# First norm of a two-block model: feature squares summed on GpSimd and ScalarE before the ones-matmul, and the first two weight splits moved

## The chip, the cores and the metric

The kernel runs on one core of one Trainium2 chip. The metric is the device time of one execution in microseconds; shown of the kernel before are three runs, of which the median counts. One more execution was taken with the hardware profiler, and every row below comes from it.

## The reference

Two transformer-like blocks work on 512 tokens of 1024 features, with 16 learned tokens put ahead of them (528 in all) in the first block. What matters here is its beginning:

```
h = concatenate([meta, x], axis=1)              # 528 tokens x 1024 features
def rms_norm(x, g):
    xf = x.astype(float32)
    y = xf * rsqrt(mean(xf * xf, axis=-1) + EPS)
    return y * g
xn = rms_norm(h, norm_mix_g)
proj = einsum('bld,de->ble', xn, w_in)          # q, k, v, forget logits, conv gates
```

After it come attention with a forget gate, a gated convolution, an output projection and an MLP, and then the second block: a state-space mixer, a gated FFN, differential attention and a second FFN. None of that is touched.

## The kernel before

Activations lie with features on the 128 partitions and tokens along the free dimension: `h` has KT = 8 feature tiles of 128 x 528. Every dense weight passes as one of 308 *units*, 128 x 1024 f32 elements (512 KB), brought by SP from `wstream` into two buffers `raw`. For precision each operand is split in two fp32r parts: ScalarE (ACT) writes `w_hi` from `raw` (`split_hi`, L375), VectorE (DVE) writes `w_lo` = `raw` - `w_hi` (`split_lo`, L379), and TensorE (PE) makes three products, hi*hi, hi*lo and lo*hi. Inputs are split the same way: `x_act` (ACT, L459) writes `x_hi` = h * gain, and `x_dve` (DVE, L465) writes `x_lo`.

The norm's factor is not applied to the input. The product is made of h * gain, and the factor `rstd`, one number per token, is multiplied in when a unit is taken out of PSUM (`wide_dve`, L564). So PE can start before the factor is known, but no bank can be emptied before it is. The first 24 units are wide ones (528 tokens, two halves of 264, so two PSUM banks each; `wide_pe`, L555) and alternate between two pairs of banks: unit n waits until unit n-2 has been taken out (`unit_ev`). Unit 0 walks the eight feature tiles k, and waits at each for its `x_lo`.

The sum of squares of the first norm is made so: GpSimd (POOL) squares the feature tiles one by one into two buffers `sq` (L1542), and PE adds them over features with matmuls against a matrix of ones (`first_stat_pe`, L423), two halves for each tile, all accumulating in one PSUM pair. Tiles 0 to 3 come ahead of unit 0, tiles 4 to 7 between the first four k steps of unit 0. Behind its squares POOL clears `aug_q` and `aug_k` (L1544 to L1547); the last of these brings `consts_ok` to 8, for which ACT waits ahead of the square root (`root_act`, L475). DVE then takes the reciprocal (`root_dve`, L480), splits the low part of unit 2, and takes out unit 0.

The order of work is written out by hand for each engine; each engine runs its own instructions in order, and semaphores tie the engines together. SP's first loads are h tiles 0 and 1, `vecs`, `ones`, h tiles 2 and 3, `raw` of unit 0, the rest of h, `raw` of unit 1. From unit 2 on, the load of unit n waits until w_lo of unit n-2 is written (`load_unit`, L364 to L369). ACT's order at the start is x_hi 0, x_hi 1, w_hi of unit 0, x_hi 2, x_hi 3, w_hi of unit 1, x_hi 4 to 7. DVE's is x_lo 0 to 2, w_lo of unit 0, x_lo 3 and 4, w_lo of unit 1, x_lo 5 to 7.

Of the kernel before, what the change touches and what calls it, by code (L numbers as in the profile page):

```python
# [10 lines left out]
ACT = mybir.ActivationFunctionType  # L11
ALU = mybir.AluOpType
# [4 lines left out]
KT = D // P  # L17
# [3 lines left out]
HALF = TOK // 2  # L21
# [103 lines left out]
def build(nc, A, out, ctx):  # L125
# [38 lines left out]
    ones = sb("ones", [P, P])  # L164
# [77 lines left out]
    ps = ctx.enter_context(nc.psum_tensor("ps", [P, 8, SEQ], F32))  # L242
# [52 lines left out]
    pool_did = sem("pool_did")  # L295
    pool = Count(pool_did)
# [74 lines left out]
    def split_hi(e, u):  # L371
        e.wait_ge(raw_in[u.c % 2], 16 * (u.round + 1))
        if not (isinstance(u.i, int) and u.n() < 4):
            e.wait_ge(unit_mm, u.n(-3))
        e.activation(w_hi[:, u.slot, :], raw[:, u.c % 2, :], ACT.Copy).then_inc(hi_ok, 1)  # L375

    def split_lo(e, u):
        e.wait_ge(hi_ok, u.n(1))
        e.tensor_tensor(w_lo[:, u.slot, :], raw[:, u.c % 2, :], w_hi[:, u.slot, :], ALU.subtract)\  # L379
            .then_inc(lo_ok, 1)  # L380
# [23 lines left out]


    STEP = {0: 0, 1: 1, 3: 2, 2: 3, 4: 4, 5: 5, 6: 6, 7: 7, 8: 8}
    SQUARES = {1: 8, 2: 16, 3: 16, 4: 32, 5: 40, 6: 48, 7: 56, 8: 64}
    SUMS = {1: 0, 2: 7, 3: 7, 4: 21, 5: 28, 6: 35, 7: 42, 8: 49}
    SUM_AT = {1: t2[:, 1, 0:SEQ], 2: t2[:, 0, 0:SEQ], 3: t2[:, 1, 0:SEQ], 4: t2[:, 1, 0:SEQ], 5: t2[:, 1, 0:SEQ],
              6: p_raw[:, 0, :], 7: t2[:, 1, 0:SEQ], 8: t2[:, 1, 0:SEQ]}  # L410
# [6 lines left out]

        return SUMS[n] + (2 * (m - 1) + (n == 2) if n in (2, 3) else m - 1)

    def first_stat_pe(e, m):  # L420
        e.wait_ge(sq_ok, m + 1)
        for half in range(2):
            last = e.matmul(ps[:, 4 + half, 0:HALF], ones[:, :], sq[:, m % 2, half * HALF:half * HALF + HALF],  # L423
                            start=(m == 0), stop=(m == KT - 1))
        last.then_inc(stat_mm, 1)

    def square_act(e, n, m, scale=1.0):

        src = h[:, m, REAL]
        if m == 0:  # L430
            e.wait_ge(stat_mm, 7 + STEP[n] if n != 2 else 7 + STEP[1])
            e.activation(SUM_AT[n], src, ACT.Square, scale=scale).then_inc(sq_ok, 1)
        else:
            k = sum_no(n, m)
            ge(e, sum_ok, k - 1)
            e.activation(sq[:, k % 2, 0:SEQ], src, ACT.Square, scale=scale).then_inc(sq_ok, 1)  # L436
# [29 lines left out]
                               ALU.subtract).then_inc(xlo_ok, 1)  # L466

    def root_act(e, n, eps, cols=SEQ):
        e.wait_ge(stat_mm, 8 + STEP[n])
        ge(e, rstd_ok, STEP[n])  # L470
        if cols > SEQ:
            o, i = halves(rt[:, :]), ps[:, 4:6, 0:HALF]
        else:
            o, i = rt[:, 0:cols], ps[:, 4, 0:cols]
        e.activation(o, i, ACT.Sqrt, bias=eps[:, 0:1], scale=1.0 / D).then_inc(rt_ok, 1)  # L475
# [65 lines left out]
    def wide_pe(e, u):  # L541

        e.wait_ge(lo_ok, u.n(1))
        if not (isinstance(u.i, int) and u.n() < 2):
            e.wait_ge(unit_ev, u.n(-1))
        b = 2 * (u.slot % 2)
        for k in range(KT):
            w = slice(k * P, (k + 1) * P)
            if isinstance(u.i, int) and u.n() == 0:
                if k < 4:  # L550
                    first_stat_pe(e, k + 4)
                e.wait_ge(xlo_ok, k + 1)
            for n, (wt, x) in enumerate(((w_hi, x_hi), (w_hi, x_lo), (w_lo, x_hi))):
                for half in range(2):
                    last = e.matmul(ps[:, b + half, 0:HALF], wt[:, u.slot, w],  # L555
                                    x[:, k, half * HALF:(half + 1) * HALF],
                                    start=(k == 0 and n == 0), stop=(k == KT - 1 and n == 2))
        last.then_inc(unit_mm, 1)

    def wide_dve(e, u, to):  # L560

# [967 lines left out]
    @block.gpsimd  # L1529
    def _(e):  # L1530
        e.memset(eps5[:, :], 1e-5).then_inc(consts_ok, 1)
        e.memset(eps6[:, :], 1e-6).then_inc(consts_ok, 1)
        e.memset(eps_o[:, :], 1e-6 / (1.0 - LAM) ** 2).then_inc(consts_ok, 1)
        e.memset(eps_f[:, :], 1e-11).then_inc(consts_ok, 1)
        e.memset(ones_e[:, :], 1e-6).then_inc(consts_ok, 1)
        e.wait_ge(consts_ok, 5)
        for m in range(KT):
            e.wait_ge(h_in[m // 2], 16)
            if m:
                e.wait_ge(sq_ok, m)  # L1540
            ge(e, stat_mm, m - 1)
            e.tensor_tensor(sq[:, m % 2, :], h[:, m, :], h[:, m, :], ALU.mult).then_inc(sq_ok, 1)  # L1542
        e.wait_ge(sq_ok, 8)
        e.memset(aug_q[:, :, :, :], 0.0).then_inc(consts_ok, 1)  # L1544
        e.memset(aug_k[:, :], 0.0).then_inc(consts_ok, 1)
        e.wait_ge(consts_ok, 7)
        e.memset(aug_k[32:40, :], 1.0).then_inc(consts_ok, 1)  # L1547
        e.wait_ge(consts_ok, 8)
        e.memset(qs[:, :, :, :], 0.0).then_inc(qz_ok, 1)
        e.memset(vp[:, :, :, :, :], 0.0).then_inc(vz_ok, 1)  # L1550
        e.memset(vm[:, :, :, :], 0.0).then_inc(vz_ok, 1)
        e.wait_ge(qz_ok, 1)
        e.wait_ge(vz_ok, 2)
        system_pool(e)
        e.wait_ge(unit_ev, 12)
        e.wait_ge(f_ok, 3)
        stage1_pool(e, 0)
        fence(e, 1)
        stage1_pool(e, 1)
        fence(e, 2)  # L1560
        e.wait_ge(hn_lo, 8)
        e.dma_start(b_in_[:, :, :, :], A["ssm_bc"][:, 0:2, :, :]).then_inc(bc_in, 16)
        e.dma_start(c_raw[:, :, :, :], A["ssm_bc"][:, 2:4, :, :]).then_inc(bc_in, 16)
        for m in range(1, KT):
            sum_pool(e, 1, m)
        tables_pool(e)
        e.drain().then_inc(tables_ok, 1)
        matrices_pool(e, 0)
        for m in range(1, KT):
            sum_pool(e, 3, m)  # L1570
            sum_pool(e, 2, m)

        def spread(u, s):
            e.wait_ge(unit_ev, u.n(1))
            m = u.n(-U_SSM)
            for q in range(4):
# [12 lines left out]
        for n in (4, 5, 6):
            for m in range(1, KT):  # L1590
                sum_pool(e, n, m)
        e.wait_ge(h_fin, 16)
        e.dma_start(onehot, A["onehot"]).then_inc(tab_in, 16)

        e.wait_ge(tab_ok, 2)
        e.dma_start(scratch, tab[0:8, :]).then_inc(tab_out, 16)
        e.memset(qs2[:, :, :, :], 0.0).then_inc(qz2_ok, 1)
        e.wait_ge(qz2_ok, 1)
        e.wait_ge(tab_out, 16)
        for p in range(8):  # L1600
            bias_load(e, p)
            if p == 0:
                e.wait_ge(hn_y, 17)
                e.wait_ge(unit_ev, U_KV + 9)
            stage2_pool(e, p)
            if p == 0:
                fence(e, 5)
        fence(e, 6)
        e.wait_ge(hn_lo, 16)
        e.dma_start(p_raw[:, :, :], A["pT"][:, 1, :, :]).then_inc(p_in, 16)  # L1610
        for n in (7, 8):
            for m in range(1, KT):
                sum_pool(e, n, m)

    @block.scalar
    def _(e):

        e.wait_ge(first_in, 32)
        for m in range(KT):
            e.wait_ge(h_in[m // 2], 16)  # L1620
            x_act(e, 0, m, "norm_mix", TOK)
            if m in (1, 3):
                split_hi(e, Unit(m // 2))
        e.wait_ge(consts_in, 16 * 7)
        e.wait_ge(consts_ok, 8)
        root_act(e, 0, eps5, TOK)
# [23 lines left out]
        for m in range(KT):  # L1650
            u = Unit(U_OUT1 + m)
# [13 lines left out]
        for s in range(16):  # L1665
# [4 lines left out]
            else:  # L1670
                m = s - 8
# [74 lines left out]
    def _(e):  # L1746
# [3 lines left out]
        e.tensor_tensor(gain_fs[:, :], vecs[:, k:k + KT], vecs[:, s:s + KT], ALU.mult).then_inc(gain_ok, 1)  # L1750
        for m in range(KT):
            x_dve(e, 0, m, "norm_mix", TOK)
            if m in (2, 4):
                split_lo(e, Unit(m // 2 - 1))
        e.wait_ge(wf_ok, 1)
        e.tensor_tensor(wf_lo[:, :, :], wf[:, :, :], wf_hi[:, :, :], ALU.subtract).then_inc(wflo_ok, 1)
        root_dve(e, 0, TOK)
# [138 lines left out]
    @block.tensor  # L1896
    def _(e):
        e.wait_ge(first_in, 32)
        for m in range(4):
            first_stat_pe(e, m)  # L1900
        units(e, U_QKVB, 4, lambda u, s: wide_pe(e, u), 1)
        f_pe(e)
        units(e, U_CU, 2, lambda u, s: wide_pe(e, u))
# [191 lines left out]
```

## Time and profile before

| what | us |
| --- | --- |
| median of three runs | 2323.01 (2322.71 to 2323.32) |
| the profiled execution, its own time | 2324.46 |
| its span, first to last instruction | 2322.7 |
| PE busy in that span | 2128.9 (92%) |
| DVE, ACT, POOL busy | 1281.0, 819.9, 466.5 |

The span leaves out what the device does around the program, 1.8 us in this execution. PE is the busiest engine and the chain of work that ended last lies on it for 84% of the span. The stretch that the change touches is the first 40 us. All start times below count from the start of the span.

### The profile page before, as it was taken

To read this page: it belongs to the slowest core of one execution; us is meant where nothing else is said; L and a number is where in the kernel's file an instruction comes from. 1 tells how busy PE (TensorE), PEld (TensorE's weight loads), DVE (VectorE), ACT (ScalarE), POOL (GpSimd) and SP (SyncE) were. 2 spreads that over 40 slices of the span, in tenths; PEclk is the share of its full clock that TensorE was granted. 3 is DMA by queue.
4 is the path that set the end of the run, shared out by engine and by line. 5 is a ranking of instruction groups with operands and counts; after the bars stand their busy time and mean duration, and the time that the engine had idled before them with its cause. 6 is when DMAs were issued, how large, how long until landed. Compare 5 with 4: busy or idle time off the path is not lost.

```text
span 2322.7 us, 27094 instructions
## 1 busy us (share of the span) xinstructions
PE 2128.9 (92%) x9788; PEld 1681.1 (72%) x9788; DVE 1281.0 (55%) x1733; ACT 819.9 (35%) x1309; POOL 466.5 (20%) x596
## 2 busy tenths in 40 slices
PE   8999999999999454799999999999977899999999
PEld 8987668888887354687787877665655577877877
DVE  4253356464355698347747466633366467556455
ACT  3123333122235345534424234432144344334233
POOL 4052017970015784010000001100131000000000
PEclk9999989999999777899999999999899899999999
DMA  4220022232322100122222323221100122323222
GB/s 141 90 73 1 1 73 91 91 100 90 100 91 74 35 1 1 65 91 82 91 99 90 109 82 104 89 69 63 59 19 10 46 82 91 109 80 106 79 98 100
DMA packets 48592, 172.16 MB, mean 74 GB/s; under 512 B 5806, under 2 KB 6318, under 8 KB 48492
## 3 DMA queue, kind: packets, MB, share of 16 engines
q1 hardware_dynamic: 47164, 166.46, 21.6%
q0 software_dynamic: 1328, 4.37, 0.6%
q8 instruction: 63, 1.03, 0.2%
q14 instruction: 37, 0.30, 0.0%
HBM read 168.68 MB, written 2.12 MB: 74 GB/s over the span
## 4 chain that ended last, share of the span: by engine, by line
PE 84%; DVE 8%; ACT 5%; issue 2%; POOL 0%; DMA 0%; DVEq 0%; SPq 0%; ACTq 0%; POOLq 0%
PE ps L393 65%; PE ps L555 6%; PE ps L517 2%; ACT sq L1061 2%; PE ps L1390 1%; PE ps L499 1%; DVE t L1075 1%; PE ps L690 1%; ACT u_t L839 1%; PE ps L691 1%; PE ps L711 1%; PE ps L1392 1%; PE ps L1410 1%; ACT t L1458 1%; PE ps L1026 1%
## 5 line engine op out<-in xcount | busy, mean ns | idle before, releaser
L393 PE MATMUL ps<-x_hi,w_hi 128*128 128x512 f32 x1280 | 513.2, 401 | 5.0 <-DVE w_lo L379 4.9
L393 PE MATMUL ps<-x_lo,w_hi 128*128 128x512 f32 x1280 | 507.1, 396 | 0.0
L393 PE MATMUL ps<-x_hi,w_lo 128*128 128x512 f32 x1280 | 506.4, 396 | 0.0
L379 DVE TENSOR_TENSOR w_lo<-raw,w_hi 128x1024 fp32r<-128x1024 f32 x308 | 395.6, 1287 | 165.1 <-ACT w_hi L375 165.1
L375 ACT ACTIVATE w_hi<-raw 128x1024 fp32r<-128x1024 f32 x308 | 321.8, 1049 | 308.0 <-PE ps L393 136.6
L393 PE MATMUL ps<-a_hi,w_hi 128*128 128x512 f32 x928 | 372.0, 401 | 19.1 <-DVEq L360 11.2
L393 PE MATMUL ps<-a_hi,w_lo 128*128 128x512 f32 x928 | 369.6, 398 | 0.0
L393 PE MATMUL ps<-a_lo,w_hi 128*128 128x512 f32 x928 | 369.5, 398 | 0.0
L393 PEld LDWEIGHTS ps<-x_hi,w_hi 128*128 128x128 f32 x1280 | 241.1, 188 | 86.4 <-issue 22.2
L445 POOL TENSOR_TENSOR t<-t,sq 128x512 f32<-128x512 f32 x49 | 71.4, 1456 | 1116.0 <-ACT sq L436 1115.0
L393 PEld LDWEIGHTS ps<-x_lo,w_hi 128*128 128x128 f32 x1280 | 241.3, 189 | 56.8 <-issue 1.7
L393 PEld LDWEIGHTS ps<-x_hi,w_lo 128*128 128x128 f32 x1280 | 241.5, 189 | 56.3
L393 PEld LDWEIGHTS ps<-a_hi,w_hi 128*128 128x128 f32 x928 | 176.8, 191 | 71.3 <-DVEq L360 11.4
L393 PEld LDWEIGHTS ps<-a_hi,w_lo 128*128 128x128 f32 x928 | 176.6, 190 | 42.1
L393 PEld LDWEIGHTS ps<-a_lo,w_hi 128*128 128x128 f32 x928 | 176.8, 191 | 41.6 <-issue 0.5
L811 DVE TENSOR_TENSOR h<-h,ps 128x512 f32<-128x512 f32 x96 | 65.8, 686 | 204.9 <-PE ps L393 204.9
L1131 ACT ACTIVATE t<-t,vecs 128x512 f32<-128x512 f32 x88 | 71.8, 816 | 241.8 <-DVE t L1159 241.8
L1165 DVE SCALAR_TENSOR_TENSOR t<-t,vecs 128x512 f32<-128x512 f32 x88 | 66.2, 752 | 75.2 <-ACT t L1131 75.2
L1159 DVE TENSOR_TENSOR t<-ps,rstd 128x512 f32<-128x512 f32 x88 | 60.8, 691 | 80.1 <-PE ps L393 79.8
L459 ACT ACTIVATE x_hi<-h,vecs 128x512 fp32r<-128x512 f32 (+1 forms) x56 | 40.0, 722 | 121.6 <-DVE h L811 109.7
L555 PE MATMUL ps<-x_hi,w_hi 128*128 128x264 f32 x384 | 79.5, 288 | 0.0
L555 PE MATMUL ps<-x_lo,w_hi 128*128 128x264 f32 x384 | 78.3, 286 | 0.0
(322 smaller groups left out, 2704.7 us busy)
## 6 DMA issues: line engine op xcount, KB each, us to landing
raw<-in_wstream SPq DMA_DIRECT2D x308, 512.0 KB, 3.3
h<-in_xT SPq DMA_DIRECT2D x4, 528.0 KB, 7.3
b_raw<-scratch POOLq DMA_DIRECT2D x8, 256.0 KB, 3.5
out<-h SPq DMA_DIRECT2D x8, 256.0 KB, 2.0
p_raw<-in_pT POOLq DMA_DIRECT2D x2, 512.0 KB, 4.6
b_in_<-in_ssm_bc POOLq DMA_DIRECT2D x1, 512.0 KB, 4.3
c_raw<-in_ssm_bc POOLq DMA_DIRECT2D x1, 512.0 KB, 6.2
vecs<-in_vecs SPq DMA_DIRECT2D x1, 294.0 KB, 3.8
```

The source lines that it names most:

```text
L375: e.activation(w_hi[:, u.slot, :], raw[:, u.c % 2, :], ACT.Copy).then_inc(hi_ok, 1)
L379: e.tensor_tensor(w_lo[:, u.slot, :], raw[:, u.c % 2, :], w_hi[:, u.slot, :], ALU.subtract)\
L393: last = e.matmul(ps[:, bank, :], wt[:, u.slot, w], x[:, k0 + k, 0:SEQ], start=(k == 0 and n == 0), stop=(k == kt - 1 and n == 2))
L445: e.tensor_tensor(SUM_AT[n], SUM_AT[n], sq[:, k % 2, 0:SEQ], ALU.add).then_inc(sum_ok, 1)
L459: e.activation(hi[:, m, 0:cols], src, ACT.Copy, scale=scale).then_inc(xhi_ok, 1)
L517: e.matmul(ps[:, 6 + k % 2, :], (spread1 if k < 8 else spread2)[:, m * P:(m + 1) * P], roots, start=True, stop=True).then_inc(hn_b, 1)
L555: last = e.matmul(ps[:, b + half, 0:HALF], wt[:, u.slot, w], x[:, k, half * HALF:(half + 1) * HALF], start=(k == 0 and n == 0), stop=(k == ...
L811: i = e.tensor_tensor(h[:, m, REAL], h[:, m, REAL], ps[:, u.slot, :], ALU.add)
L1061: e.activation(dst, u_t[32 * j:32 * j + 32, 4 * m + q, :], ACT.Gelu_apprx_tanh).then_inc(ge_ok, 1)
L1131: e.activation(t1[:, s % 2, 0:SEQ], t0[:, s % 2, 2:SEQ + 2], ACT.Identity, bias=vec(f"ffn_b{layer}", c), scale=vec(f"ffn_w{layer}", 88 + c ...
L1159: e.tensor_tensor(t0[:, s % 2, 2:SEQ + 2], ps[:, u.slot, :], rstd[:, 0:SEQ], ALU.mult).then_inc(unit_ev, 1)
L1165: n = dve.did(e.scalar_tensor_tensor(y, t0[:, s % 2, 1:SEQ + 1], vec(f"ffn_w{layer}", 44 + c), y, ALU.mult, ALU.add))
```

## The change

The sum over feature tiles is taken off PE. POOL keeps a running sum `SUM_0` (in `t1[:, 1, :]`): it squares tile 0 straight into it, squares tiles 2, 4 and 6 into `sq[:, 0, :]`, and ACT squares tiles 1, 3, 5 and 7 into `sq[:, 1, :]`; POOL adds each of the seven to the sum. ACT's square of tile m waits for POOL's sum over tile m-2, since both use one buffer. One pair of matmuls against ones, behind unit 0, adds over the partitions. On ACT, w_hi of unit 1 goes behind everything else of this stage; on DVE, w_lo of unit 0 goes ahead of x_lo 2, and w_lo of unit 1 behind x_lo 7. The counts of `sq_ok` and `stat_mm` in later norms are lowered to match and say nothing new.

```diff
+    SUM_0 = t1[:, 1, :]
+    def first_square_act(e, m):
+        if m > 1:
+            e.wait_ge(sum0_ok, m - 1)
+        e.activation(sq[:, 1, :], h[:, m, :], ACT.Square).then_inc(sq0_ok, 1)
+    def first_sum_pool(e, m):
+        if m == 0:
+            e.tensor_tensor(SUM_0, h[:, m, :], h[:, m, :], ALU.mult).then_inc(sum0_ok, 1)
+            return
+        if m % 2:
+            e.wait_ge(sq0_ok, m // 2 + 1)
+        else:
+            e.wait_ge(sum0_ok, m - 1)
+            n = pool.did(e.tensor_tensor(sq[:, 0, :], h[:, m, :], h[:, m, :], ALU.mult))
+            e.wait_ge(pool_did, n)
+        e.wait_ge(sum0_ok, m)
+        e.tensor_tensor(SUM_0, SUM_0, sq[:, m % 2, :], ALU.add).then_inc(sum0_ok, 1)
-    def first_stat_pe(e, m):
-        e.wait_ge(sq_ok, m + 1)
+    def first_stat_pe(e):
+        e.wait_ge(sum0_ok, KT)
         for half in range(2):
-            last = e.matmul(ps[:, 4 + half, 0:HALF], ones[:, :], sq[:, m % 2, half * HALF:half * HALF + HALF],
-                            start=(m == 0), stop=(m == KT - 1))
+            last = e.matmul(ps[:, 4 + half, 0:HALF], ones[:, :], SUM_0[:, half * HALF:half * HALF + HALF],
+                            start=True, stop=True)
         last.then_inc(stat_mm, 1)
...
-                if k < 4:
-                    first_stat_pe(e, k + 4)
                 e.wait_ge(xlo_ok, k + 1)
...
         last.then_inc(unit_mm, 1)
+        if isinstance(u.i, int) and u.n() == 0:
+            first_stat_pe(e)
...
         for m in range(KT):
             e.wait_ge(h_in[m // 2], 16)
-            if m:
-                e.wait_ge(sq_ok, m)
-            ge(e, stat_mm, m - 1)
-            e.tensor_tensor(sq[:, m % 2, :], h[:, m, :], h[:, m, :], ALU.mult).then_inc(sq_ok, 1)
-        e.wait_ge(sq_ok, 8)
+            first_sum_pool(e, m)
...
             x_act(e, 0, m, "norm_mix", TOK)
-            if m in (1, 3):
-                split_hi(e, Unit(m // 2))
+            if m == 1:
+                split_hi(e, Unit(0))
+            if m % 2:
+                first_square_act(e, m)
+        split_hi(e, Unit(1))
...
             x_dve(e, 0, m, "norm_mix", TOK)
-            if m in (2, 4):
-                split_lo(e, Unit(m // 2 - 1))
+            if m == 1:
+                split_lo(e, Unit(0))
+        split_lo(e, Unit(1))
...
         e.wait_ge(first_in, 32)
-        for m in range(4):
-            first_stat_pe(e, m)
```

POOL's work between its first constants and the clearing of `aug_q`, before:

```order
L1542 TENSOR_TENSOR sq<-h 128x528 [waits h_in0,consts_ok]
L1542 TENSOR_TENSOR sq<-h 128x528 [waits sq_ok,h_in0]
L1542 TENSOR_TENSOR sq<-h 128x528 [waits stat_mm,sq_ok,h_in1] x2
L1542 TENSOR_TENSOR sq<-h 128x528 [waits stat_mm,sq_ok,h_in2] x2
L1542 TENSOR_TENSOR sq<-h 128x528 [waits stat_mm,sq_ok,h_in3] x2
L1544 MEMSET aug_q 128x2048 [waits sq_ok]
```

and the same stretch of POOL in the changed kernel (`t` is the running sum):

```order
L433 TENSOR_TENSOR t<-h 128x528 [waits h_in0,consts_ok]
L442 TENSOR_TENSOR t<-t,sq 128x528 [waits sum0_ok,sq0_ok,h_in0]
L439 TENSOR_TENSOR sq<-h 128x528 [waits sum0_ok,h_in1]
L442 TENSOR_TENSOR t<-t,sq 128x528 [waits sum0_ok,pool_did]
L442 TENSOR_TENSOR t<-t,sq 128x528 [waits sum0_ok,sq0_ok,h_in1]
L439 TENSOR_TENSOR sq<-h 128x528 [waits sum0_ok,h_in2]
L442 TENSOR_TENSOR t<-t,sq 128x528 [waits sum0_ok,pool_did]
L442 TENSOR_TENSOR t<-t,sq 128x528 [waits sum0_ok,sq0_ok,h_in2]
L439 TENSOR_TENSOR sq<-h 128x528 [waits sum0_ok,h_in3]
L442 TENSOR_TENSOR t<-t,sq 128x528 [waits sum0_ok,pool_did]
L442 TENSOR_TENSOR t<-t,sq 128x528 [waits sum0_ok,sq0_ok,h_in3]
L1564 MEMSET aug_q 128x2048
```

Eight squares have become four squares and seven additions, and the clearing of `aug_q` stands behind all eleven. On ACT the first instructions of the changed kernel are

```order
L483 ACTIVATE x_hi<-h,vecs 128x528 [waits first_in]
L483 ACTIVATE x_hi<-h,vecs 128x528 [waits h_in0]
L377 ACTIVATE w_hi<-raw 128x1024 [waits raw_in0]
L428 ACTIVATE sq<-h 128x528
L483 ACTIVATE x_hi<-h,vecs 128x528 [waits h_in1] x2
L428 ACTIVATE sq<-h 128x528 [waits sum0_ok]
L483 ACTIVATE x_hi<-h,vecs 128x528 [waits h_in2] x2
L428 ACTIVATE sq<-h 128x528 [waits sum0_ok]
L483 ACTIVATE x_hi<-h,vecs 128x528 [waits h_in3] x2
L428 ACTIVATE sq<-h 128x528 [waits sum0_ok]
L377 ACTIVATE w_hi<-raw 128x1024 [waits raw_in1]
```

Four squares are new there, three of them wait for POOL, and the first stands behind w_hi of unit 0; w_hi of unit 1 stood behind x_hi 3 before. DVE's stretch, where L489 is `x_lo` and L381 `w_lo`, now reads

```order
L489 SCALAR_TENSOR_TENSOR x_lo<-h,vecs,x_hi 128x528 [waits xhi_ok] x2
L381 TENSOR_TENSOR w_lo<-raw,w_hi 128x1024 [waits hi_ok]
L489 SCALAR_TENSOR_TENSOR x_lo<-h,vecs,x_hi 128x528 [waits xhi_ok] x6
L381 TENSOR_TENSOR w_lo<-raw,w_hi 128x1024 [waits hi_ok]
L1780 TENSOR_TENSOR wf_lo<-wf,wf_hi 128x64 [waits wf_ok]
L504 RECIPROCAL rstd<-rt 128x528 [waits rt_ok]
```

where before three x_lo, w_lo, two x_lo, w_lo and three x_lo stood ahead of `wf_lo`.

## Rows read from the trace of the kernel before

**Rows 1.** The page's busy times: engine, us, share of the span, instructions

```profile
PE 2128.9 (92%) x9788; PEld 1681.1 (72%) x9788; DVE 1281.0 (55%) x1733; ACT 819.9 (35%) x1309; POOL 466.5 (20%) x596
```

**Rows 2.** The chain that ended last, 0 to 60 us: start, length, what

```profile
19.41 0.89 PE ps L423 x4
20.30 0.73 PE ps L555 x6
...
21.92 38.09 PE ps L555 x313
```

**Rows 3.** Timeline of DVE, 25 to 44 us: start, length, instruction, [idle before <-releaser]

```profile
25.65 3.45 DVE L480 RECIPROCAL rstd<-rt 128x528 f32<-128x528 f32 x1
29.13 1.23 DVE L379 TENSOR_TENSOR w_lo<-raw,w_hi 128x1024 fp32r<-128x1024 f32 x1
30.27 0.70 DVE L564 TENSOR_TENSOR qkvb<-ps,rstd 128x528 f32<-128x528 f32 x1
...
37.29 0.71 DVE L564 TENSOR_TENSOR qkvb<-ps,rstd 128x528 f32<-128x528 f32 x1 [1.21 <-PE ps L555]
...
43.13 0.71 DVE L564 TENSOR_TENSOR qkvb<-ps,rstd 128x528 f32<-128x528 f32 x1 [4.00 <-PE ps L555]
```

**Rows 4.** Timeline of ACT, 9 to 26 us

```profile
9.73 1.06 ACT L375 ACTIVATE w_hi<-raw 128x1024 fp32r<-128x1024 f32 x1 [2.47 <-DMA raw<-in_wstream]
...
23.33 1.28 ACT L475 ACT_TABLE_LOAD   x1 [5.53 <-POOL aug_k L1547]
24.62 0.70 ACT L475 ACTIVATE rt<-ps,eps 128x528 f32<-128x528 f32 x1
```

**Rows 5.** Timeline of POOL, 8 to 24 us

```profile
8.55 1.06 POOL L1542 TENSOR_TENSOR sq<-h 128x528 f32<-128x528 f32 x1 [1.60 <-DMA h<-in_xT]
...
18.85 1.48 POOL L1542 TENSOR_TENSOR sq<-h 128x528 f32<-128x528 f32 x1 [1.20 <-PE ps L423]
20.39 1.81 POOL L1544 MEMSET aug_q<- 128x2048 f32 x1
...
22.73 0.53 POOL L1547 MEMSET aug_k<- 8x528 f32 x1
```

**Rows 6.** Timeline of POOL and of DVE in short windows, 11.4 to 15.7 us

```profile
11.63 1.51 POOL L1542 TENSOR_TENSOR sq<-h 128x528 f32<-128x528 f32 x1 [0.64 <-PE ps L423]
13.27 1.87 POOL L1542 TENSOR_TENSOR sq<-h 128x528 f32<-128x528 f32 x1
...
11.45 0.77 DVE L465 SCALAR_TENSOR_TENSOR x_lo<-h,vecs,x_hi 128x528 fp32r<-128x528 f32 x1 [3.26 <-ACT x_hi L459]
12.13 2.09 DVE L379 TENSOR_TENSOR w_lo<-raw,w_hi 128x1024 fp32r<-128x1024 f32 x1
14.14 1.56 DVE L465 SCALAR_TENSOR_TENSOR x_lo<-h,vecs,x_hi 128x528 fp32r<-128x528 f32 x1
```

**Rows 7.** Later norms' sum (L445) and square (L436): durations ns min/median/max

```profile
L445 POOL TENSOR_TENSOR t<-t,sq x49: 1287/1302/2368, 325.7 to 2274.4; 128x512 f32<-128x512 f32 x49
...
L436 ACT ACTIVATE sq<-h x49: 612/615/621, 325.0 to 2273.7; 128x512 f32<-128x512 f32 x49
```

**Rows 8.** Timeline of PE, 14 to 18 us, around the start of unit 0

```profile
14.28 2.04 PE L423 MATMUL ps<-sq,ones 128*128 128x264 f32 x4 [1.93 <-DVE w_lo L379]
15.74 1.02 PE L555 MATMUL ps<-x_hi,w_hi 128*128 128x264 f32 x2
...
17.44 1.24 PE L423 MATMUL ps<-sq,ones 128*128 128x264 f32 x4
```

**Rows 9.** Stretches: length, busy us of PE, PEld, DVE, ACT, POOL; PEclk, DMA share, GB/s

```profile
1708.50:1710.00 1.50, 0.00 (x0) 0.00 (x0) 0.30 (x1) 1.44 (x5) 0.00 (x0) 1.00 0.02 5
1710.80:1714.20 3.40, 3.40 (x12) 2.49 (x11) 1.83 (x6) 0.54 (x2) 0.00 (x0) 0.50 0.00 0
...
1741.00:1743.00 2.00, 0.00 (x0) 0.00 (x0) 0.70 (x2) 1.51 (x5) 0.00 (x0) 1.00 0.00 0
1743.20:1746.60 3.40, 3.36 (x19) 2.51 (x20) 2.10 (x7) 0.80 (x2) 0.00 (x0) 1.00 0.02 5
```

More of the change, by code:

```diff
@@ L255, in build @@
     sum_ok = sem("sum_ok")
+    sq0_ok = sem("sq0_ok")
+    sum0_ok = sem("sum0_ok")
     gain_ok = sem("gain_ok")
@@ L406, in build @@
     STEP = {0: 0, 1: 1, 3: 2, 2: 3, 4: 4, 5: 5, 6: 6, 7: 7, 8: 8}
-    SQUARES = {1: 8, 2: 16, 3: 16, 4: 32, 5: 40, 6: 48, 7: 56, 8: 64}
+    SQUARES = {1: 0, 2: 8, 3: 8, 4: 24, 5: 32, 6: 40, 7: 48, 8: 56}
     SUMS = {1: 0, 2: 7, 3: 7, 4: 21, 5: 28, 6: 35, 7: 42, 8: 49}
@@ L430, in square_act @@
         if m == 0:
-            e.wait_ge(stat_mm, 7 + STEP[n] if n != 2 else 7 + STEP[1])
+            e.wait_ge(stat_mm, STEP[n] if n != 2 else STEP[1])
             e.activation(SUM_AT[n], src, ACT.Square, scale=scale).then_inc(sq_ok, 1)
@@ L468, in root_act @@
     def root_act(e, n, eps, cols=SEQ):
-        e.wait_ge(stat_mm, 8 + STEP[n])
+        e.wait_ge(stat_mm, 1 + STEP[n])
         ge(e, rstd_ok, STEP[n])
```

## The prediction

> **What bounds the kernel now.** I read first the busy times: PE works 92% of the span [rows 1], so a microsecond of PE idle time is normally a microsecond of the kernel. Then the chain that ended last: PE waits for w_lo of unit 0 until 14.28 us [rows 8], and from then on the chain stays on it without a break, 38.09 us in one piece from 21.92 [rows 2]. So what delays PE ahead of about 40 us moves the whole rest, and what shortens PE's work there gains only if nothing else is late.
>
> The timelines of the other engines show how much can be late. Units are taken out by DVE at 37.29 (unit 2) and 43.13 (unit 3), each as soon as PE is done, so a wide unit takes 5.84 us of PE, and unit 2, which ended 0.04 before 37.29, began at 37.25 - 5.84 = 31.41 us [rows 3]. It needs the banks of unit 0, and those were taken out at 30.27 + 0.70 = 30.97 us [rows 3]. **The slack is 0.44 us.** That taking out hangs on a chain without a gap: POOL's last square ends at 18.85 + 1.48 = 20.33; it clears `aug_q` and twice `aug_k` until 23.26 [rows 5]; ACT, released by the last clearing after 5.53 us of waiting, loads a table and takes the root [rows 4]; DVE takes the reciprocal, splits the low part of unit 2 and takes out unit 0 [rows 3]. From POOL's last square to the free banks it is 30.97 - 20.33 = 10.64 us. The reader is to see that the norm's chain, which seems to be hidden, was within half a microsecond of being the bound.
>
> **The change part by part.** Call T the time at which POOL ends its last instruction of the norm (20.33 before). All of the 10.64 us behind it stays as it is and in the same order. The pair of ones-matmuls that now stands behind unit 0 starts with T too, but takes 0.89 us at full clock [rows 2] and 17.44 - 15.74 = 1.70 us is the most that six matmuls of such a width took at the lower level [rows 8], so it ends ahead of the clearings (2.93 us). Hence unit 2 starts at T + 10.64 + 0.05, and against 31.41 the change costs **T - 20.72**, if PE has nothing to do in between.
>
> *PE's own work.* Seven of eight pairs go. The four ahead of unit 0 lay beside waiting for the weights and are worth nothing. The four inside unit 0 took 15.74 - 14.28 = 1.46 us (the first, at the lower clock) and about 0.89 each, some 4.1 us together [rows 2, 8], and unit 0 can start when w_lo of unit 0 is done, about 12.1 instead of 14.28. PE gains about 6 us ahead of unit 1. It gets none of it, if T is late: unit 1 then waits behind the pair, and unit 2 for the banks. I cost this gain at nothing; the cover is the norm's chain.
>
> *T, from rows.* POOL's sum can't go on from tile 0 before ACT has squared tile 1, which stands behind w_hi of unit 0 (start 9.73, idle before it ended by the DMA [rows 4]). It ends at 10.79, and a square takes 0.62 us [rows 7]. So POOL is idle until about 11.45, though tile 2 is there at 8.55 [rows 5]. Behind that come seven additions and three squares. A square takes 1.06 us with DVE idle [rows 5]; an addition has a median of 1.30 us at 512 columns and a largest of 2.37 [rows 7], 1.33 with 528. Ten of them alone: 7 x 1.33 + 3 x 1.06 = 12.5 us. **Lower bound: T = 24.0**, cost +3.2 us.
>
> But DVE works beside it, and the rows show that two such instructions don't run at once. From 11.45 on: x_lo of DVE, which alone takes 0.77; the square of POOL issued at 11.63 ends at 13.14; w_lo, issued at 12.13, takes 2.09 instead of 1.23 [rows 3]; the next square is issued at 13.27 and takes 1.87 instead of 1.06; the next x_lo takes 1.56 [rows 6]. Counting each back from its end by what it takes alone, they start at 11.45, 12.08, 13.00, 14.08 and 14.93: one after the other, with turns of 0.63 (x_lo), 0.9 (square) and 1.08 (w_lo); an addition is then 1.33 - 0.17 = 1.16. With these turns I walk through the changed order. w_lo of unit 0 holds until 11.9; addition 1 to 13.1; x_lo 2; square 2 to 14.6; x_lo 3; addition 2 to 16.3; x_lo 4; addition 3 to 18.1; x_lo 5; square 4 to 19.6; x_lo 6 (its x_hi stands on ACT behind the square of tile 5, which waits for addition 3); addition 4 to 21.5; x_lo 7; addition 5 to 23.3; square 6 to 24.2; addition 6 to 25.6; w_lo of unit 1, whose w_hi waited on ACT behind the square of tile 7 until 25.2, to 26.7; addition 7, ends at **28.0**. I take 28.0, since these five rows are the nearest to what will happen; that costs 28.0 - 20.72 = **+7.3 us**. If the hand-overs that lie bare (four semaphores between POOL's own instructions, 0.1 us each) and full durations count, it is 29.5 and +8.8: the upper bound.
>
> The Trainium skill (SBUF — State Buffer, Who interferes with whom) says that the second port pair of VectorE and GpSimd is an exclusive lock for the whole instruction. By that rule T is 28.0 to 29.5 as above; by the other reading of the same rows, a mean slowing of POOL of 0.44 us for each of ten instructions, it would be 28.4.
>
> The Trainium skill (GPSIMD Engine Reference, Performance versus the Vector engine) gives two-input operations 2.6 cycles an element whatever they compute, an estimate of 1.14 us for 528 elements at 1.2 GHz. By that the seven additions would be 1.3 us shorter together and the cost +6.0 us; the rows show 1.30 against 1.06, and I go by them.
>
> *Other queues.* ACT's w_hi of unit 1 moves to about 24; w_lo of unit 1 ends at 26.8, ahead of T, so unit 1 is not held by it but by the pair. SP's load of unit 3 waits for it and goes out at 27; its w_hi stands on ACT behind the root, the table loads and w_hi of unit 2, no sooner than T + 6. The load of unit 4 waits for w_lo of unit 2, which keeps its distance to T. No other DMA moves. POOL's later work for the state-space parameters shifts by as much as PE does. Nothing there.
>
> *PE's clock.* PE stands idle from about 20 us, when unit 0 ends, to T, and again ahead of unit 2: unit 1 starts at about 29.2, takes 5.84 to 7.4 and ends at 35 to 36.7, unit 2 starts at 38.7, so 2 to 3.6 us idle. A lower clock in unit 1 is hidden by that wait. In unit 2 it counts: PE's step at 15.74, behind 1.93 us idle, took 1.70 us where one at full clock takes 0.73 [rows 2, 8]; behind two pauses of PE late in the kernel, of which 1.5 and 2.0 us are shown, the granted clock was 0.50 (1.2 GHz) for 3.4 us once, and 1.00 (2.4 GHz) once [rows 9]. So this is 0 to 1.6 us, and I take the middle, 0.8.
>
> Sum: +7.3 + 0.8 = +8.1 us. The profiled execution of 2324.46 (span 2322.7) lies 1.45 above the median; the difference holds for either, and on the median it gives 2323.0 + 8.1 = **2331.1 us**.
>
> **The rivals.** (1) *No taking of turns*: additions and squares run as if alone. For it: the median of 49 additions, 1.302, is hardly over the least, 1.287 [rows 7], so most of those didn't wait. Against it: all five rows of 11.45 to 15.70. Time 2323.0 + 3.2, to 2327.8 with the clock's term. (2) *PE's relief decides*, and the kernel gets faster: the banks would be free in time, and up to 6 us of PE's gain come through, 2317. Its place is POOL between 11.45 and T, and it decides from T under 20.72, which asks 0.93 us for each of ten instructions, less than the fastest square of the trace. That excludes it but for squares of ACT coming much earlier than the weights' DMA lets them. (3) *The clock stays low*: behind 8 us of idle and a second wait, all of unit 2 runs slow, at most 8 x (1.70 - 0.73) = 7.8 us more [rows 2, 8], half of it likelier: 2323.0 + 7.3 + 3.9 = 2334.2. (4) The change does what it says; the order of instructions shows all of it, and I give nothing to its not doing so.
>
> **How the numbers follow.** Forecast (turns are taken, T = 27 to 29.5, clock 0 to 1.6: 2329.3 to 2333.4): 0.72. Rival 1, with all that lies between it and the forecast: 0.16. Rival 2: 0.03. Rival 3: 0.09. The range takes rival 1's upper half and the nearer part of rival 3: 2327 to 2334. A measurement can tell 0.2% or 4.6 us from no change; slower by more than that begins at 2327.7. Slower has the forecast, rival 3 and a little of rival 1: 0.84; within 0.2%: 0.13; faster: 0.03.
>
> **What would show it.** In the profile after: POOL's eleven instructions with additions well above 1.33 us where DVE's x_lo lie beside them, and its last ending at 27 to 29.5; ACT's table load 3.0 us behind that; DVE's first L588 near 38; a pause of PE ahead of the pair of 6 us or more and one of 1 to 4 us ahead of unit 2, named as waiting for DVE. I am wrong if the last addition ends before 25 us, if PE doesn't pause ahead of unit 2, or if the shift of unit 2 doesn't reach the end of the kernel.

## The result, and the profile after

The changed kernel takes 2334.26 us (median of six runs, 2333.12 to 2337.36) against 2323.16 us of the kernel before (median of six, 2322.62 to 2327.58): 11.1 us slower, ratio 1.0048 with a 95% interval of 1.0035 to 1.0061. Forecast were 2331.1 and a range of 2327 to 2334. It went the way that was forecast; the time lies just outside the range.

The profiled execution took 2337.36 us, the highest of the six, with a span of 2335.6. POOL's timeline from the first square on:

```profile
4.54 1.06 POOL L433 TENSOR_TENSOR t<-h 128x528 f32<-128x528 f32 x1 [3.46 <-DMA h<-in_xT]
11.59 1.76 POOL L442 TENSOR_TENSOR t<-t,sq 128x528 f32<-128x528 f32 x1 [5.98 <-ACT sq L428]
13.31 1.53 POOL L439 TENSOR_TENSOR sq<-h 128x528 f32<-128x528 f32 x1
14.92 1.65 POOL L442 TENSOR_TENSOR t<-t,sq 128x528 f32<-128x528 f32 x1
16.74 1.57 POOL L442 TENSOR_TENSOR t<-t,sq 128x528 f32<-128x528 f32 x1 [0.17 <-POOL t L442]
...
24.43 1.30 POOL L442 TENSOR_TENSOR t<-t,sq 128x528 f32<-128x528 f32 x1
25.90 2.06 POOL L442 TENSOR_TENSOR t<-t,sq 128x528 f32<-128x528 f32 x1 [0.17 <-POOL t L442]
27.91 1.80 POOL L1564 MEMSET aug_q<- 128x2048 f32 x1
```

Where [rows 5] show the last square ending at 20.33, the last addition now ends at 27.96. Six us of that are plain waiting for ACT's square of tile 1. The addition at 24.43, with VectorE idle when it starts, takes 1.30; the ones at 14.92 and 16.74, between two x_lo, take 1.65 and 1.57, and the last one, beside w_lo of unit 1, takes 2.06. ACT and DVE behind it:

```profile
30.84 1.28 ACT L499 ACT_TABLE_LOAD   x1 [5.88 <-POOL aug_k L1567]
32.13 0.70 ACT L499 ACTIVATE rt<-ps,eps 128x528 f32<-128x528 f32 x1
```

```profile
33.15 3.45 DVE L504 RECIPROCAL rstd<-rt 128x528 f32<-128x528 f32 x1
36.63 1.23 DVE L381 TENSOR_TENSOR w_lo<-raw,w_hi 128x1024 fp32r<-128x1024 f32 x1
37.78 0.70 DVE L588 TENSOR_TENSOR qkvb<-ps,rstd 128x528 f32<-128x528 f32 x1
...
44.72 0.71 DVE L588 TENSOR_TENSOR qkvb<-ps,rstd 128x528 f32<-128x528 f32 x1 [1.15 <-PE ps L577]
```

The same chain as in [rows 3, 4], shifted whole: table load +7.51, unit 0 taken out +7.51, unit 2 taken out 37.29 to 44.72, +7.43. And PE, with the three places where it now waits:

```profile
12.29 0.78 PE L577 MATMUL ps<-x_hi,w_hi 128*128 128x264 f32 x2 [12.29 <-DVE w_lo L381]
...
22.81 0.41 PE L577 MATMUL ps<-x_hi,w_lo 128*128 128x264 f32 x2
28.02 2.13 PE L447 MATMUL ps<-t,ones 128*128 128x264 f32 x4 [4.80 <-POOL t L442]
29.57 1.01 PE L577 MATMUL ps<-x_hi,w_hi 128*128 128x264 f32 x2
...
38.62 0.48 PE L577 MATMUL ps<-x_hi,w_hi 128*128 128x264 f32 x2 [2.06 <-DVE qkvb L588]
```

Unit 0 starts 3.4 us sooner than in [rows 8] and ends at 23.2; then PE idles 4.8 us for the sum, and 2.06 us more for unit 0's banks. A wide unit is 24 such lines, eight tiles with three products each, and counted so the kernel before starts unit 2 at 31.25 and unit 3 at 37.09:

```profile
31.25 0.40 PE L555 MATMUL ps<-x_hi,w_hi 128*128 128x264 f32 x2
...
37.09 0.40 PE L555 MATMUL ps<-x_hi,w_hi 128*128 128x264 f32 x2
```

So unit 2 starts 38.62 - 31.25 = 7.4 us later. The chain that ended last, followed back through the first 60 us, now names POOL, which it didn't name at all before (there PE's two lines had 68.1% and 8.1%):

```profile
by line: PE ps L577 35.6%; POOL t L442 19.4%; DMA raw<-in_wstream 12.0%; POOL sq L439 6.7%; DVE rstd L504 5.6%; POOL aug_q L1564 2.9%; issue 2.9%; ACT L499 2.1%; DVE w_lo L381 2.0%; ACT w_hi L377 1.8%; SPq L1532 1.4%; DVE qkvb L588 1.0%; AC
```

The shift of 7.43 us stays to a hundredth until the first attention, whose first matmul starts at 178.03 instead of 170.59. But at the end the profiles lie 12.9 us apart. These further 5.5 us are what the experiments had to explain.

### The profile page after: what moved, and what is told of

Same layout as the page of the kernel before. It is cut to its first block, busy times and chain, and to the rows that moved or that the text cites. A ratio compares the mean times of both kernels' runs of the same rounds, so it can differ in the third digit from the quotient of the medians.

```text
span 2335.6 us, 27047 instructions
## 1 busy us (share of the span) xinstructions
PE 2129.5 (91%) x9760; PEld 1683.7 (72%) x9760; DVE 1282.0 (55%) x1733; ACT 822.2 (35%) x1313; POOL 472.8 (20%) x599
## 4 chain that ended last, share of the span: by engine, by line
PE 83%; DVE 8%; ACT 5%; issue 2%; POOL 1%; DMA 0%; DVEq 0%; SPq 0%; POOLq 0%; ACTq 0%
PE ps L395 65%; PE ps L577 6%; PE ps L541 2%; ACT sq L1085 2%; PE ps L1414 1%; PE ps L523 1%; DVE t L1099 1%; PE ps L714 1%; ACT u_t L863 1%; PE ps L715 1%; PE ps L735 1%; PE ps L1434 1%; PE ps L1416 1%; ACT t L1482 1%; DVE rstd L504 1%
## 5 line engine op out<-in xcount | busy, mean ns | idle before, releaser
L381 DVE TENSOR_TENSOR w_lo<-raw,w_hi 128x1024 fp32r<-128x1024 f32 x308 | 392.8, 1278 | 169.9 <-ACT w_hi L377 169.9
L395 PEld LDWEIGHTS ps<-a_hi,w_hi 128*128 128x128 f32 x928 | 177.6, 191 | 71.3 <-DVEq L362 11.4
```

The source lines that it names most:

```text
L395: last = e.matmul(ps[:, bank, :], wt[:, u.slot, w], x[:, k0 + k, 0:SEQ], start=(k == 0 and n == 0), stop=(k == kt - 1 and n == 2))
```

## The experiments

Two theories stood against each other. **A**: the change costs what it delays the emptying of unit 0's banks; the rest is the clock's doing. **B**: something else of the change costs further time. There were eleven runs, of eight different kernels besides the two compared. This table sums them up; each is told below. The columns of the profile give how much later than in the first profile of the kernel before one and the same instruction starts: unit 2's first matmul (31.25 there); the first matmul of the first attention (170.59); VectorE's first copy into `qkvb` in that attention (205.79); one of its reciprocals near the end of the differential attention (1799.08); and the end (2322.7). A star marks the profiles in which PE didn't wait for unit 0's banks. The last column is the ratio of the timed runs, its interval in brackets, and in us of 2323.

| kernel | unit 2 | attention | 205.79 | 1799.08 | end | ratio |
| --- | --- | --- | --- | --- | --- | --- |
| the change | +7.4 | +7.4 | +11.9 | +9.4 | +12.9 | 1.0048 [1.0035, 1.0061] = +11.1 |
| the change again (e5) | +7.5 | +7.6 | +7.6 | +7.5 | +7.4 | 1.0043 [1.0030, 1.0056] = +10.0 |
| before + 4 clearings (e1) | +7.1 | +8.8 | +12.9 | +13.9 | +14.2 | 1.0044 [1.0030, 1.0058] = +10.2 |
| the change, clearings early (e4) | +7.0 | +7.1 | +7.1 | +7.1 | +7.0 | 1.0030 [1.0018, 1.0043] = +7.0 |
| the change, square first (e11) | +3.3 | +4.9 | +4.5 | +4.1 | +3.8 | 1.0017 [1.0008, 1.0026] = +4.0 |
| the change without x_lo 2 to 7 (e2) | +5.8 | +5.9 | +8.0 | +10.3 | +10.2 | one run |
| before + 2 clearings (e8) | +2.5 | +5.1 | +4.8 | +7.4 | +7.2 | 1.0029 [1.0019, 1.0040] = +6.7 |
| the sum alone (e6) | +7.9 | +9.5 | +9.1 | +11.8 | +11.7 | 1.0045 [1.0033, 1.0057] = +10.5 |
| the splits alone (e3) | -2.7* | -2.7 | -3.1 | -0.6 | +2.7 | 0.9992 [0.9983, 1.0001] = -1.9 |
| the splits alone again (e10) | -3.0* | -3.0 | -0.8 | +1.5 | +1.7 | 0.9987 [0.9978, 0.9995] = -3.0 |
| splits and clearings early (e7) | -1.0* | -1.0 | +1.3 | +3.9 | +3.6 | 1.0000 [0.9992, 1.0009] = 0.0 |
| before, again (e9) | +0.7* | +0.7 | +2.8 | +5.2 | +5.4 | 0.9999 [0.9990, 1.0007] = -0.2 |

**The delay by itself (e1, e8).** Nothing of the change, only four, or two, clearings more on POOL:

```diff
         e.wait_ge(sq_ok, 8)
+        for t in (qs, vp, qs, vp, qs, vp)[:4]:
+            e.wait_ge(pool_did, pool.did(e.memset(t[:], 0.0)))
         e.memset(aug_q[:, :, :, :], 0.0).then_inc(consts_ok, 1)
```

> The kernel before, with four clearings of 128x2048 (1.81 us each and a semaphore of about 0.07) put on GpSimd between its last square and the clearing of aug_q; nothing else. Theory A (the change costs what it delays the emptying of unit 0's banks, and all that follows is a matter of where the rest of the kernel then lies in time): GpSimd's norm end moves from 20.33 to about 27.9, unit 2 starts at 38.3 to 38.8 instead of 31.41, and the median moves by what it moved by in the change, +9 to +13 us. Theory B (the 3.5 us that the change costs beyond the 7.4 of unit 2 come from the change's own instructions): unit 2 starts at the same time, but the median moves by +7 to +8 only.

Unit 2 started at 38.32, and the ratio was 1.0044, +10.2 us: a loss of the change's size is there without any of its instructions. That alone doesn't decide between the theories, since the interval, +7.0 to +13.5 us, holds B's 7 to 8 too, and since this run had a cost that the change has not. In its profile the clock was low in unit 2:

```profile
38.32 0.78 PE L555 MATMUL ps<-x_hi,w_hi 128*128 128x264 f32 x2 [6.79 <-DVE qkvb L564]
38.90 0.64 PE L555 MATMUL ps<-x_lo,w_hi 128*128 128x264 f32 x2
39.34 0.64 PE L555 MATMUL ps<-x_hi,w_lo 128*128 128x264 f32 x2
```

A pair takes 0.44 us there against 0.24 at the full clock, unit 2 takes 1.7 us longer, and the attention starts 8.8 us late instead of 7.1. In the change, where PE had been idle for 2.06 us rather than 6.79, the clock stayed up in unit 2 in both profiles.

> The kernel before with two clearings of 128x2048 put between GpSimd's last square and the clearing of aug_q. GpSimd's norm chain then moves by 3.7 us less what the squares end earlier or later. Theory A (what delays GpSimd delays unit 2 one for one beyond a slack of 0.44 us, and nothing else): unit 2 starts at 34.3 to 34.9 instead of 31.41 (+2.9 to +3.5, or 1.6 more where the clock is low in it), and the median moves by +2 to +5. Theory B (a delay of the start costs more than itself later on): the median moves by +6 or more.

POOL's last square ended at 19.2 here, so the bank chain shifted by 2.6 us only and unit 2 started at 33.75, +2.5. A low clock, behind 3.82 us of idle PE, made +5.1 of it, and the median moved by 7.7 us (2331.72 of eight runs), by ratio 6.7. That is beyond theory A's 5 and meets theory B's 6 or more: a delay of the start did cost more than itself, 2.6 us of it through the clock in unit 2. In the profiles part of unit 2 ran at the low clock behind 3.4, 3.6, 3.8 and 6.8 us of idle PE (e11, e6, e8, e1), at 1.6, 1.6, 2.6 and 1.7 us more, and at the full clock behind 1.2 to 2.1 us (e2, e4 and the change, twice).

**Taking turns (e2).** x_lo of tiles 2 to 7 is left out of the first norm:

```diff
-            x_dve(e, 0, m, "norm_mix", TOK)
+            if m < 2:
+                x_dve(e, 0, m, "norm_mix", TOK)
+            else:
+                e.wait_ge(xhi_ok, m + 1)
+                e.memset(x_lo[:, m, :].bitcast(F32), 0.0).then_inc(xlo_ok, 1)
```

> The changed kernel, with x_lo of tiles 2 to 7 of the first norm not computed: VectorE clears these tiles instead (one output, no input from memory), with the same waits and semaphores. Theory A (GpSimd and VectorE take turns for instructions with two inputs): the additions beside the clearings fall to about 1.3 us, GpSimd's last addition ends at 24.3 to 25.8 instead of 27.96, unit 2 starts 2 to 3.5 us earlier. Theory B (GpSimd's additions of 528 columns simply take about 1.6 us here): the end stays at 27.5 to 28.

POOL's rows:

```profile
12.22 1.76 POOL L442 TENSOR_TENSOR t<-t,sq 128x528 f32<-128x528 f32 x1 [6.46 <-ACT sq L428]
13.94 1.06 POOL L439 TENSOR_TENSOR sq<-h 128x528 f32<-128x528 f32 x1
15.08 1.31 POOL L442 TENSOR_TENSOR t<-t,sq 128x528 f32<-128x528 f32 x1
16.57 1.31 POOL L442 TENSOR_TENSOR t<-t,sq 128x528 f32<-128x528 f32 x1 [0.17 <-POOL t L442]
...
24.36 2.07 POOL L442 TENSOR_TENSOR t<-t,sq 128x528 f32<-128x528 f32 x1 [0.17 <-POOL t L442]
```

Additions beside clearings fell from about 1.65 to 1.31 us and squares from 1.53 to 1.06; only the first and last, beside DVE's two w_lo, stayed at 1.76 and 2.07. So the stretching comes from VectorE's instructions with two inputs in memory, where a clearing has none, and not from additions as such, as turns would have it. The weights came later in this run, and the chain began 0.63 us later; from the first addition's start to the last one's end it took 14.2 us instead of 16.4. **Turns for x_lo cost 2.2 us, not more.** The end, 26.43, lies above my 25.8 by just the 0.63 us of the later start. Unit 2 started at 37.08, 1.5 us sooner than in the change.

**The two halves of the change (e3, e10, e6).** e3 and e10 are one kernel, before with nothing but the split order of the change (the lines of `split_hi` and `split_lo` in the diff above); e6 is the change with these lines undone.

> The kernel before, with only the two weight splits moved as in the change. Theory A (the sum on GpSimd is the whole cost): TensorE's unit 0 starts at about 12.3 to 13, GpSimd's last square ends within 1 us of 20.3, unit 2 starts within 1.5 us of 31.4, the median moves by less than 2 us. Theory B (w_hi and w_lo of unit 1 at the end of their queues delay unit 1 and cost part of the loss): unit 1 starts later than 25.6 and the median moves by +1 to +4 us.

> The kernel before with only the two weight splits moved, once more. Unit 2 starts at 28.2 to 29.2 (2.2 to 3.2 us sooner than before). Theory A (the gain at unit 2 reaches the end, under scatter): the two comparisons together give -1 to -3.5 us. Theory B (a start that is sooner costs as much again later): 0 to +1.

> The changed kernel with the two weight splits back where they stood before: only the sum on GpSimd and ScalarE is left of the change. Theory A (GpSimd's chain of eleven with turns for VectorE is the bound; the splits only take their turns at other places): GpSimd's last addition ends at 27 to 29.5, unit 2 starts at 37.7 to 40.2, the median is within 2 us of the change's. Theory B (w_hi of unit 1 at the end of ScalarE's queue and w_lo in front of the last addition are what makes the end late): the last addition ends at 25 to 26.5 and unit 2 starts 1.5 to 3 us sooner than in the change.

With the splits alone POOL's squares end at 17.5, PE never stops, and unit 0's banks are free at 28.16:

```profile
13.20 1.13 PE L423 MATMUL ps<-sq,ones 128*128 128x264 f32 x4 [0.80 <-POOL sq L1542]
13.97 0.60 PE L555 MATMUL ps<-x_hi,w_hi 128*128 128x264 f32 x2
```

```profile
27.46 0.70 DVE L564 TENSOR_TENSOR qkvb<-ps,rstd 128x528 f32<-128x528 f32 x1
```

Unit 0's first pair of products starts 1.8 us sooner than in [rows 8], and at full clock: PE stood idle for 0.80 us ahead of the ones-matmuls with which unit 0 begins, instead of 1.93. That is more than either theory of e3 had: the squares end 2.8 us sooner than 20.33 where A had at most 1, and unit 2 starts 2.7 us sooner where A had at most 1.5. The attention starts 2.7 and 3.0 us sooner, and the second comparison's interval (0.9978 to 0.9995) excludes 1. The first one's (0.9983 to 1.0001) does not. Half of the change thus was a gain, of some 2 to 3 us at the attention, and the fastest kernel here is that half alone. With the sum alone POOL's last addition ended at 28.49 and unit 2 started at 39.16, both a little later than in the whole change. So the sum is the whole of the loss, and theory B of e6 falls.

**The clearings (e4, e7).** e4 is the change with the clearings of `aug_q` and `aug_k` moved into POOL's idle time behind tile 0; e7 is the kernel before with the splits moved and the clearings behind tile 1. The moved block, in e4:

```diff
             first_sum_pool(e, m)
-        e.memset(aug_q[:, :, :, :], 0.0).then_inc(consts_ok, 1)
-        e.memset(aug_k[:, :], 0.0).then_inc(consts_ok, 1)
-        e.wait_ge(consts_ok, 7)
-        e.memset(aug_k[32:40, :], 1.0).then_inc(consts_ok, 1)
+            if m == 0:
+                e.memset(aug_q[:, :, :, :], 0.0).then_inc(consts_ok, 1)
+                e.memset(aug_k[:, :], 0.0).then_inc(consts_ok, 1)
+                e.wait_ge(consts_ok, 7)
+                e.memset(aug_k[32:40, :], 1.0).then_inc(consts_ok, 1)
+                e.wait_ge(consts_ok, 8)
```

> The changed kernel, with the three clearings of aug_q and aug_k moved to GpSimd's idle time behind the square of tile 0. Theory A (the chain from the last addition over the clearings to the root is the bound): the last addition still ends at 27.5 to 28.5, the root's table load starts behind the ones-matmuls at about 29.6 instead of 30.84, unit 2 starts about 1.3 us earlier, the median is 1 to 2 us below the change's, +8 to +10 us against before. Theory B (the ones-matmuls' end, not the clearings, released the root): no difference to the change.

The last addition ended at 28.16, and the root was released by PE instead of POOL:

```profile
30.44 1.28 ACT L499 ACT_TABLE_LOAD   x1 [5.30 <-PE ps L447]
```

Only 0.40 us sooner than 30.84: the pair of ones-matmuls, at the low clock behind 4.81 us of idle PE, lasts 2.13 us (1.05 at the full one, timed in the same way), and nearly fills the place of the clearings. Unit 2 started at 38.26. The median, 2331.81, and the ratio 1.0030 (1.0018 to 1.0043, +7.0 us) lie below the change's, by more than 0.4 us explains; the intervals overlap.

> The kernel before, with the two weight splits moved as in the change, and the clearings of aug_q and aug_k moved into GpSimd's idle time behind the square of tile 1. Theory A (with the splits moved TensorE is the bound again: in that run unit 0's banks came free 0.5 us ahead of unit 2): unit 2 starts at 28.3 to 29.3 as with the splits alone, the banks come free 1.5 to 3 us ahead, the median is -3 to 0 us against before and no better than with the splits alone. Theory B (the clearings were still in the way): unit 2 starts sooner than 28.0.

No gain: ratio 1.0000 (0.9992 to 1.0009), and the attention 1.0 us sooner than before instead of 2.7 to 3.0. The root was released by PE again, at 21.04, half a microsecond later than with the splits alone: the clearings pushed POOL's third square from 8.6 to 9.8 and so the ones-matmuls behind them. PE does the last twelve ahead of unit 0's products in one piece from 10.91, and these products start at 15.71, as late as before, instead of 13.97. Unit 2 starts at 30.27, a microsecond later than theory A had it.

**Where POOL's chain starts (e11).** The change, with ACT's square of tile 1 ahead of w_hi of unit 0:

```diff
             x_act(e, 0, m, "norm_mix", TOK)
+            if m % 2:
+                first_square_act(e, m)
             if m == 1:
                 split_hi(e, Unit(0))
-            if m % 2:
-                first_square_act(e, m)
```

> The changed kernel, with ScalarE's square of tile 1 ahead of w_hi of unit 0 instead of behind it. Theory A (GpSimd's chain of eleven starts when that square is there, so it starts with the inputs and not with the weights): the first addition starts at 7.8 to 8.6 instead of 11.59, the last ends at 24 to 26 instead of 27.96, unit 2 starts at 34.7 to 36.8 (or 1.6 later with a low clock in it), the median is 2 to 4 us below the change's. Theory B (the chain is bound by what comes later, ScalarE's squares or VectorE's turns): the last addition ends at 27 or later.

```profile
7.91 1.34 POOL L442 TENSOR_TENSOR t<-t,sq 128x528 f32<-128x528 f32 x1 [2.19 <-ACT sq L428]
...
22.28 1.57 POOL L442 TENSOR_TENSOR t<-t,sq 128x528 f32<-128x528 f32 x1 [0.17 <-POOL t L442]
23.79 1.80 POOL L1564 MEMSET aug_q<- 128x2048 f32 x1
```

Two lines in another order on ACT took 4.1 us off POOL's end (23.85), somewhat more than forecast; unit 2 started at 34.51, the ratio was 1.0017 (1.0008 to 1.0026, +4.0 us), 6 to 7 us below the change's where 2 to 4 were expected. The profile shows only 2.6 us of that at the attention, since PE stood idle for 3.41 us ahead of unit 2 and ran part of it at the low clock, 1.6 us more. It is still slower than before.

**The scatter (e5, e9).** The change again, and the kernel before against itself.

> The changed kernel once more, beside fresh runs of the kernel before. Theory A (the change costs the 7.4 us by which unit 2 starts later, and the rest of the first comparison's 11.1 us is scatter of the clock's low stretches, the median of before having been taken from a narrow low group): the difference of the medians is +7 to +10 us, and the individual times of either kernel spread over 4 to 6 us. Theory B (a second, steady loss of 3.5 us in the later kernel): +10.5 to +12 again. Unit 2 starts at 38.3 to 39.2 in either case, or 1.5 later where the clock is low in it.

> The kernel before against itself, for the scatter. Theory A (the place of the clock's low stretches scatters the total of one and the same kernel): the ratio is 1.000 within 0.001, individual times spread over 4 us or more, and this second profile has all instruction starts up to 160 us within 0.5 us of the first one's, while its end lies 0 to 6 us off, in step with its low-clock time (211 us in the first). Theory B (the totals of the kernel before are steady and low): its end lies within 1 us of the first profile's.

The change again gave 2332.49 against 2324.05 (20 runs), +8.4 us by medians, 1.0043 by ratio, and its times spread from 2331.9 to 2339.5. Its profile is the key: the same kernel, unit 2 at 38.74, the attention at 178.16 (+7.57), and an end only 7.4 us behind the first profile of before, where the first profile of the change ended 12.9 behind. Against that profile of before nothing is lost from the attention on, at any of the marks in the table. The kernel before, profiled again, has its attention 0.7 us later (I had expected at most 0.5) and its end 5.4 us later than in its first profile; its 12 runs spread from 2322.9 to 2329.9.

Where the further time goes can be seen by timing the same work. From the first matmul of the attention to VectorE's copy (205.79 in the first profile of before), in the first and the second profile of before, and in the first and the second of the change:

```profile
170.59:205.79 35.20, 33.81 (x187) 26.11 (x188) 11.88 (x38) 11.74 (x38) 7.48 (x8) 0.84 0.00 0
171.25:208.62 37.37, 35.99 (x187) 27.68 (x188) 11.98 (x38) 11.74 (x38) 7.48 (x8) 0.79 0.00 0
178.03:217.69 39.66, 38.28 (x187) 29.04 (x188) 12.06 (x38) 11.74 (x38) 7.48 (x8) 0.74 0.00 0
178.16:213.36 35.20, 33.81 (x187) 26.12 (x188) 11.89 (x38) 11.74 (x38) 7.49 (x8) 0.84 0.00 0
```

The first figure behind the window is its length, the last but two the granted clock. The same 187 matmuls take 35.20, 37.37, 39.66 and 35.20 us, at a clock of 0.84, 0.79, 0.74 and 0.84. This stretch alone put 4.5 us between the two profiles of the change, and 2.2 us between the two of one unchanged kernel. A second one lies behind 1799.08, at the end of the differential attention; the first profile of before, and the first and the second of the change:

```profile
1800.14:1813.13 12.99, 9.62 (x34) 3.08 (x34) 1.45 (x3) 7.48 (x11) 0.00 (x0) 1.00 0.01 2
1809.55:1826.02 16.47, 13.11 (x34) 5.11 (x34) 1.45 (x3) 7.48 (x11) 0.00 (x0) 0.69 0.00 0
1807.63:1820.63 13.00, 9.62 (x34) 3.09 (x34) 1.44 (x3) 7.48 (x11) 0.00 (x0) 1.00 0.00 1
```

Here it is 3.5 us, at 0.69 instead of 1.00. The splits alone (e3), whose attention started 2.7 us early, took 16.45 us at 0.69 for the same work. So the first profile's 12.9 us are 7.4 of delay and 4.5 and 3.5 from two low stretches, less 2.5 given back between them. I had expected the end to go in step with the total of low clock; for e9 it did not, since its mean clock of 0.955 is that of the first profile. It matters where the low stretches fall, not only how long they are.

## Why the prediction was wrong in its size

**The chain, right to 0.1 us.** The walk through the order gave 28.0 us for POOL's last addition; it is 27.96, and 28.08 in the second profile, and each of the ten steps ended within 0.3 us of the walk. The 10.64 us behind it gave 38.64 for the banks and 38.7 for unit 2; measured are 38.48 and 38.62. What was in the walk by luck: I had the hand-overs at nothing and the last w_lo as an ordinary turn; the rows show 0.17 us before three additions, and the turns for x_lo shorter in sum, 2.2 us.

**The start of unit 2 before, wrong by 0.16 us.** I worked it out as 37.25 - 5.84 = 31.41. But 5.84 us is the distance between the starts of two units (31.25 and 37.09), and 37.25 the end of unit 2's last matmul, which overlaps the first one of unit 3. So the slack was 0.28 us and not 0.44, the cost T - 20.56, and the forecast at unit 2 with it +7.4, which is what was measured (+7.4 and +7.5).

**PE's work costed at nothing: right, by another course.** I had unit 0 end at about 20 us and PE idle for 6 us or more ahead of the ones-matmuls. Unit 0 ended at 23.2 instead of 25.6, since it waited for x_lo at each of its last three tiles (0.37, 0.54 and 0.75 us), and the pause was 4.8 us. Nothing of the gain came through. But I had put no number on the gain that the split order has by itself. It is 2 to 3 us at the attention (e3, e10), hidden in the change, shown only with the sum taken away. That is not a wrong term of the sum, but the most useful thing that the diff held, and the text passed it over.

**The rivals.** With turns (e2) and without relief for PE it went as weighed. Rival 3, a low clock in unit 2, is real where PE stood idle for longer (e1, e6, e8, e11), but cost 1.6 to 2.6 us there and not 3.9 to 7.8.

**The step that failed: PE's clock, 0 to 1.6 us, in unit 2 alone.** The sum ended with "+0.8" for it, and put what the clock does behind unit 2 at nothing, without a reason. In the change's two profiles unit 2 had the full clock, so that this term was 0, and the cost up to the attention 7.4 and 7.6 us. The timed runs give 11.1 and 10.0. The 2.4 to 3.7 us between lie behind the start of the attention, where the sum had no term at all. What profiles show there is one and the same kernel taking 4.5 us more or less for a part of the first attention, and 3.5 for a part of the differential one, with the granted clock (0.74 against 0.84, 0.69 against 1.00). The range was built as if the only clock term were the one next to the change. The base was not at fault here: 2323.0 was forecast from and 2323.16 measured beside the change. But it was luck. The three runs shown of before lie within 0.6 us of one another (2322.71 to 2323.32), and I took them for its median; in the 29 runs of the last comparison that is 2325.42, with a spread of 2322.4 to 2329.8. Three runs that agree closely don't show the spread of a kernel.

**What stays open.** A delay of 7.4 to 7.6 us at the attention lies below the first comparison's interval (8.1 to 14.2 us) and just inside the second's (7.0 to 13.0). The fastest run of the change lies 10.1 us above the fastest of before in the same comparison (2331.86 and 2321.76), so scatter about one common loss of 7.5 is hardly the whole account: on the average over runs the change seems to lose some 3 us more behind the start of the attention than before does. For the other kernels the ratio lies between 0.9 us below the shift of their attention and 1.6 us above it. Whether the change's attentions lie in an unfavourable place of the clock's pattern, or this is chance of six runs each, the runs don't tell.

## What to carry to other kernels

Before moving work off the busiest engine, measure the slack of the chain that it goes to. Here PE could lose seven matmul pairs, but the norm's chain had 0.28 us to spare, and four squares and seven additions in sequence on GpSimd took 7.6 us more than eight squares whose sum PE made on the side. A chain of dependent instructions should start with its first input, and not behind a wait for something else in the same queue: two lines in another order made its end 4.1 us sooner.

Take a change that moves several things apart before it is judged. Its cheap part (the order of two splits) was a gain, its clever part the loss.

Where a stage's clock differs from run to run, compare profiles at marks ahead of and behind that stage, each the same instruction in both and not the same time, and let the totals come from many runs.

## What the runs showed of the hardware that I had not expected

GpSimd and VectorE take turns so strictly that a schedule could be worked out from it here: five rows of before gave the end of a chain of ten instructions to 0.1 us, and each step to 0.3 us. The Trainium skill (SBUF — State Buffer, Who interferes with whom) calls it an exclusive lock, and the rows agree: 1.31 us for an addition beside VectorE's clearings, 1.57 to 1.70 beside x_lo, 1.76 and 2.06 beside w_lo.

The pair of ones-matmuls behind 4.8 us of idle PE took 2.13 us; with PE at work it takes 1.05. So this short work, alone at the end of a chain, cost twice its time, just where it was waited for; in e4 that ate 1.1 us of what moving the clearings would have given.
